# 56 late modulation chunks as VectorE products in the feed-forward stage instead of TensorE products

## The reference

```python
def _ada(cond, l, P):
    return (jax.nn.silu(cond) @ P['w_ada'][l] + P['b_ada'][l])[:, None, :]

def _layer(x, mod, l, P, pos, ctx):
    sm, scm, gm, sf, scf, gf = jnp.split(mod, 6, axis=-1)
    h = _rmsnorm(x, P['norm_mix_g'][l]) * (1 + scm) + sm
    a, own = _mixer(h, l, P, pos, ctx)
    x = x + gm * a
    h = _rmsnorm(x, P['norm_ffn_g'][l]) * (1 + scf) + sf
    f = _swiglu(h, ...) if l % 2 == 0 else _moe(h, l // 2, P)
    return x + gf * f, own
```

## Time and profile before

| | |
|---|---|
| median of 3 runs | 2117.39 us (2114.71 to 2118.08) |
| profiled execution, first to last instruction | 2115.9 us |
| granted TensorE clock, mean | 0.997 of full speed (2.4 GHz) |
| TensorE busy | 2061.1 us (97%) |
| VectorE busy | 1356.0 us (64%) |
| ScalarE busy | 1147.1 us (54%) |
| HBM traffic | 210 GB/s over the span |

### The profile page before, as it was taken

How to read it: one execution, slowest core, us unless ns; L and a number is a source line. 1 busy time by engine, 2 the same in 40 slices (tenths; PEclk the granted TensorE clock), 3 DMA queues, 4 the chain that set the end, 5 groups by cost and what they waited for, 6 DMA issues and landing times. The chain is left out here.

```text
span 2115.9 us, 31825 instructions
## 1 busy us (share of the span) xinstructions
PE 2061.1 (97%) x12214; PEld 1792.1 (85%) x12214; DVE 1356.0 (64%) x1435; ACT 1147.1 (54%) x1412; POOL 191.3 (9%) x186
## 2 busy tenths in 40 slices
PE   8999999999999999999999999999999999999997
PEld 4898568999999999989856887888888888888885
DVE  5427533643423444653853358988998889988898
ACT  5217544322212223532754347787877777878775
POOL 1130000000000000012000026200000000000003
PEclk9999999999999999999999999999999999999999
DMA  9220154234323222322024339999999999999996
GB/s 324 84 86 6 62 183 136 80 100 140 105 78 97 64 62 75 109 81 67 6 77 163 101 113 406 408 408 386 388 379 390 380 380 379 373 385 382 386 388 199
DMA packets 275056, 445.24 MB, mean 210 GB/s; under 512 B 11952, under 2 KB 158736, under 8 KB 274928
## 3 DMA queue, kind: packets, MB, share of 16 engines
q1 hardware_dynamic: 264480, 412.58, 54.4%
q0 software_dynamic: 8752, 30.09, 3.8%
q10 hardware_dynamic: 1728, 1.21, 0.2%
HBM read 428.34 MB, written 16.62 MB: 210 GB/s over the span
## 5 line engine op out<-in xcount | busy, mean ns | idle before, releaser
L1872 DVE TENSOR_TENSOR w_lo<-mraw,w_hi 128x1792 fp32r<-128x1792 f32 (+2 forms) x306 | 643.5, 2114 | 88.3 <-ACT w_hi L1226 87.1
L1226 ACT ACTIVATE w_hi<-mraw 128x1792 fp32r<-128x1792 f32 (+2 forms) x306 | 541.7, 1776 | 173.2 <-PE ps L2594 160.8
L2592 PE MATMUL ps<-w_hi,xs_lo 128*128 128x448 f32 (+1 forms) x816 | 310.6, 381 | 4.0 <-DVE w_lo L1872 2.9
L2594 PE MATMUL ps<-w_hi,xs_hi 128*128 128x448 f32 (+1 forms) x816 | 305.9, 375 | 0.0
L2593 PE MATMUL ps<-w_lo,xs_hi 128*128 128x448 f32 (+1 forms) x816 | 305.6, 374 | 0.0
L1348 DVE TENSOR_TENSOR sub_lo<-zone,sub_hi 128x1024 fp32r<-128x1024 f32 (+2 forms) x112 | 129.5, 1158 | 217.7 <-ACT sub_hi L909 217.7
L2592 PEld LDWEIGHTS ps<-w_hi,xs_lo 128*128 128x128 f32 x816 | 153.4, 188 | 30.3 <-DVE w_lo L1872 10.6
L1591 DVE TENSOR_REDUCE stat<-ps 128x2 f32<-128x1536 f32 (+3 forms) x80 | 92.3, 1156 | 121.7 <-PE ps L2275 100.9
L2594 PEld LDWEIGHTS ps<-w_hi,xs_hi 128*128 128x128 f32 x816 | 153.3, 188 | 19.7
L2593 PEld LDWEIGHTS ps<-w_lo,xs_hi 128*128 128x128 f32 x816 | 153.5, 188 | 18.7
L2143 PE MATMUL ps<-f_hi,sub_lo 128*128 128x320 f32 x704 | 162.7, 312 | 1.7 <-issue 1.7
(11 more groups left out here) (360 smaller groups left out, 3540.0 us busy)
## 6 DMA issues: line engine op xcount, KB each, us to landing
mraw<-in_moe_w_down SPq DMA_DIRECT2D x68, 1024.0 KB, 9.1
mraw<-in_moe_w_gate SPq DMA_DIRECT2D x68, 896.0 KB, 7.9
mraw<-in_moe_w_up SPq DMA_DIRECT2D x68, 896.0 KB, 7.4
zone<-in_w_ada SPq DMA_DIRECT2D x48, 1024.0 KB, 5.8
mraw<-in_moe_w_gate SPq DMA_DIRECT2D x34, 1024.0 KB, 7.9
mraw<-in_moe_w_up SPq DMA_DIRECT2D x34, 1024.0 KB, 9.5
mraw<-in_moe_w_down SPq DMA_DIRECT2D x34, 768.0 KB, 9.8
zone<-in_w_in SPq DMA_DIRECT2D x13, 1024.0 KB, 5.3
```

The lines of the kernel that those rows point to most:

```text
L1226: nc.scalar.activation(w_hi[:, n % SPLITS, a], mraw[:, n % MRING, a], ACT.Copy).then_inc(w_hi_ready, 1)
L1872: nc.vector.tensor_tensor(w_lo[:, n % SPLITS, a], mraw[:, n % MRING, a], w_hi[:, n % SPLITS, a].bitcast(f32), ALU.subtract).then_inc(w_spl ...
L2592: nc.tensor.matmul(out, a_lo, b_hi, start=start, stop=False)
L2594: return nc.tensor.matmul(out, a_hi, b_hi, start=False, stop=stop)
```

## The change

Layer 0's chunks 16 to 39 stay on TensorE (6 pairs, steps 0 to 12 of the attention of layer 0). The other 56 chunks, 40-47 of layer 0 and all 48 of layer 1, are computed by VectorE in the feed-forward stage of layer 0. The host lays their weights output-major: a chunk is 128 partitions (outputs) by 1024 inputs, and two chunks make a piece of 1 MB ("mods", 28 pieces, rows of 4 KB in memory). Both conditioning vectors are copied to all partitions by a DMA on ScalarE's queue in layer 0's second attention, and ScalarE applies SiLU to them (128 x 2048) at the start of the feed-forward stage. For each chunk VectorE does two products with a running sum, one for each vector, 112 in all, each 128 x 1024; the sum starts from the bias and goes right into `mod`. One chunk follows the low part in each of a block's two halves of VectorE's work; two chunks follow the low parts at each of columns 0 to 5 of the first half's down products. The pieces go into the same ring. Waits that named the old semaphores name the new one.

```diff
+ADA_COLS = 40 * P
+ADA_PAIRS = in_pairs([(0, c) for c in range(8, 20)])
+MODS = [(0, c) for c in range(40, 48)] + [(1, c) for c in (*range(8, 16), *range(8), *range(16, 48))]
+MODS_DOWN = 6
+def mods_at_down(d):
+    return len(FF_HALF[0]) + d
+def mods_at(j):
+    return j if j < len(FF_HALF[0]) else j + MODS_DOWN
 def weight_pieces():
...
-        for pair in ADA_PAIRS[l]:
+        for pair in ADA_PAIRS if l == 0 else ():
             out += [("ada", *p) for p in pair]
...
                     out += [("gate", j // 2), ("up", j // 2)]
-                    out += [("ada", *p) for p in ADA_FFN.get(j, ())]
-                out += [("down", half, d) for d in range(KC)]
+                    out += [("mods", mods_at(j)), ("mods", mods_at(j + 1))]
+                for d in range(KC):
+                    out.append(("down", half, d))
+                    if half == 0 and d < MODS_DOWN:
+                        out.append(("mods", mods_at_down(d)))
 def piece_freed(n):
...
+    if PIECES[n][0] == "mods":
+        return "mod_rows", 4 * (PIECES[n][1] + 1)
...
+                if kind[0] == "mods":
+                    sp.dma_start(slot.rearrange("p (c k) -> p c k", c=2), w_mods[:, 2 * kind[1]:2 * kind[1] + 2]).then_inc(arrival, 16)
+                    return
...
-            sp.wait_ge(mod_late, TURNS_BEFORE[1] + len(ADA_PAIRS[1]) // 2)
+            sp.wait_ge(mod_rows, 2 * len(MODS))
...
-                    pool.wait_ge(late_turned, TURNS_BEFORE[l])
+                    pool.wait_ge(mod_rows, 2 * len(MODS))
...
+                    if l == 0:
+                        act.dma_start(cond_rows.rearrange("p c k -> p (c k)"), d["cond_rows"].partition_broadcast(P)).then_inc(vec_in, 16)
...
                     root(4, token_scale)
+                    act.wait_ge(vec_in, 48)
+                    nc.scalar.activation(cond_rows, cond_rows, ACT.Silu).then_inc(cond_ready, 1)
...
+                def row_mods(m, i):
+                    n = PIECE_AT["mods", m]
+                    to, c = MODS[2 * m + i]
+                    dve.wait_ge(cond_ready, 2)
+                    dve.wait_ge(*piece_arrival(n))
+                    w = piece_place(n)[:, D_MODEL * i:D_MODEL * (i + 1)]
+                    b = V_BADA + 48 * to + c
+                    if m or i:
+                        dve.wait_ge(mod_rows, 4 * m + 2 * i - 1)
+                    for g in range(2):
+                        nc.vector.tensor_tensor_reduce(mod_parts if g == 0 else w, w, cond_rows[:, g], 1.0, vecs[:, b:b + 1],
+                                                       ALU.mult, ALU.add, mod[:, to, c, g:g + 1]).then_inc(mod_rows, 1)
...
                             sub_rest(q + 1 + (j == 0))
-                            if j - 1 in ADA_FFN:
-                                ffn_rows_turned(j - 1)
-                            if j - 2 in ADA_FFN and ffn_pair(j - 2) % 2:
-                                ffn_mods(j - 2)
+                            row_mods(mods_at(j), 0)
...
                             if j:
                                 sub_rest(q + 1)
+                            row_mods(mods_at(j), 1)
...
                                 sub_rest(q + 1)
+                            if half == 0 and d_ < MODS_DOWN:
+                                for i in range(2):
+                                    row_mods(mods_at_down(d_), i)
+                            if half == 0 and d_ == 0:
+                                dve.wait_ge(mod_rows, mods_before([(0, c) for c in range(40, 48)]))
                             residual(l, ("down", half, d_), d_, 40)
...
-                                if u == "gate" and j - 1 in ADA_FFN:
-                                    ffn_ada(j - 1)
-                                if u == "gate" and j - 2 in ADA_FFN and ffn_pair(j - 2) % 2:
-                                    ffn_turn(j - 2)
```

More of the change, by code:

```diff
@@ L86, with mods_before @@
 ADA_FIRST = (0, 2, 1, 3)
[L87 to L94, removed]
+ADA_COLS = 40 * P
+ADA_PAIRS = in_pairs([(0, c) for c in range(8, 20)])
+MODS = [(0, c) for c in range(40, 48)] + [(1, c) for c in (*range(8, 16), *range(8), *range(16, 48))]
+MODS_DOWN = 6
+def mods_before(chunks):
+    return 2 * (max(MODS.index(m) for m in chunks) + 1)
+def mods_at_down(d):
+    return len(FF_HALF[0]) + d
+def mods_at(j):
+    return j if j < len(FF_HALF[0]) else j + MODS_DOWN
 def weight_pieces():
@@ L310, in build @@
     w_ada = d["w_ada"].rearrange("l (k p) n -> l p k n", p=P)
+    w_mods = d["w_mods"].rearrange("c p k -> p c k")
     w_in = d["w_in"].rearrange("l (k p) n -> l p k n", p=P)
@@ L450, in build @@
         token_scale, up_part = spare[:, 0:T], spare[:, T:2 * T]
-        late_rows_t = arena[:, ATT + 1024 + RING * RING_F:ATT + 2048 + RING * RING_F].rearrange("p (u n) -> p u n", u=2)
+        cond_rows = arena[:, ATT + 1024 + RING * RING_F:ATT + 1024 + RING * RING_F + 2 * D_MODEL].rearrange("p (c k) -> p c k", c=2)
+        mod_parts = spare[:, 2 * T:2 * T + D_MODEL]
         shift_part = stat.rearrange("p i n -> p (i n)")[:, 0:8].rearrange("p (s u c) -> p s u c", s=2, u=2)
@@ L527, in build @@
         cond_ready, lam_exp, lam_prod_ready, mod_ready = sem("cond_ready"), sem("lam_exp"), sem("lam_prod_ready"), sem("mod_ready")
-        mod_late = sem("mod_late")
+        mod_late, mod_rows = sem("mod_late"), sem("mod_rows")
         ada_rows_done, ada_rows, late_rows, late_rows_done = sem("ada_rows_done"), sem("ada_rows"), sem("late_rows"), sem("late_rows_done")
@@ L806, in _ @@
                     pool.dma_start(slot_tokens, d["no_tokens"]).then_inc(no_tokens, 16)
-            pool.wait_ge(late_rows_done, PAIRS_BEFORE[1] + len(ADA_PAIRS[1]))
+            pool.wait_ge(late_rows_done, len(ADA_PAIRS))
+            pool.wait_ge(prompt_q, HEADS * DEPTH)
             nc.gpsimd.tensor_copy(router32, router_w[:]).then_inc(router_ready, 1)
@@ L1140, in _ @@
                     if k == 0:
-                        act.wait_ge(mod_late, TURNS_BEFORE[l] + len(ADA_PAIRS[l]) // 2)
+                        act.wait_ge(*((mod_rows, 2 * len(MODS)) if l else (mod_late, len(ADA_PAIRS) // 2)))
                     if l:
@@ L1655, in late_mods @@
                 def late_mods(v):
-                    dve.wait_ge(late_turned, TURNS_BEFORE[l] + v + 1)
-                    add_bias(l, 2 * ADA_PAIRS[l][2 * v][0][1], 8, ps[:, ADA_AT:ADA_AT + 16]).then_inc(mod_late, 1)
+                    dve.wait_ge(late_turned, v + 1)
+                    add_bias(0, 2 * ADA_PAIRS[2 * v][0][1], 8, ps[:, ADA_AT:ADA_AT + 16]).then_inc(mod_late, 1)
                 def late_rows_turned(u):
-                    dve.wait_ge(late_rows_done, PAIRS_BEFORE[l] + u + 1)
+                    dve.wait_ge(late_rows_done, u + 1)
                     nc.vector.transpose(ada_rows_t[:, u % 2], ps[:, ADA_AT:ADA_AT + 512]).then_inc(late_rows, 1)
@@ L1675, in beside @@
                         turned_lo(*turn_at(i - 1), turns_before(i - 1))
+                    if l or i // 5 >= len(ADA_PAIRS) // 2:
+                        return
                     if i % 5 == 1:
@@ L1687, in _ @@
                 sub_rest(q + 1)
-                dve.wait_ge(mod_late, TURNS_BEFORE[l] + len(ADA_PAIRS[l]) // 2)
+                dve.wait_ge(*((mod_rows, 2 * len(MODS)) if l else (mod_late, len(ADA_PAIRS) // 2)))
                 make_gain(l, 1)
@@ L1771, in _ @@
                                 sub_rest(q + 1)
+                            row_mods(mods_at(j), 1)
                         if half:
-                            dve.wait_ge(mod_late, TURNS_BEFORE[1])
+                            dve.wait_ge(mod_rows, mods_before([(1, c) for c in range(16)]))
                             make_gain(1, 0)
@@ L2420, in late_ada @@
                 def late_ada(u):
[L2422 to L2425, removed]
+                    pe.wait_ge(late_rows, u)
+                    pe.wait_ge(mod_late, u // 2)
+                    for p in ADA_PAIRS[u]:
                         ada(*p, ps[:, ADA_AT:ADA_AT + 512])
@@ L2429, in late_turn @@
                 def late_turn(v):
-                    pe.wait_ge(late_rows, PAIRS_BEFORE[l] + 2 * v + 2)
+                    pe.wait_ge(late_rows, 2 * v + 2)
                     sum_groups(ada_rows_t, ps[:, ADA_AT:ADA_AT + 16])
@@ L2435, in first @@
                 def first(i):
-                    if i % 5 == 4:
+                    if l == 0 and i % 5 == 4 and i // 5 < len(ADA_PAIRS) // 2:
                         late_turn(i // 5)
                 def beside(i):
-                    if i % 5 in (0, 2):
+                    if l == 0 and i % 5 in (0, 2) and i // 5 < len(ADA_PAIRS) // 2:
                         late_ada(2 * (i // 5) + (i % 5 == 2))
@@ L2455, in _ @@
                 else:
-                    pe.wait_ge(mod_late, TURNS_BEFORE[1] + len(ADA_PAIRS[1]) // 2)
+                    pe.wait_ge(mod_rows, 2 * len(MODS))
                     for c in range(2):
@@ L2468, in _ @@
```

(6 more changed lines are left out.)

## The result

The changed kernel takes 2131.05 us (median of 4 runs, 2130.58 to 2132.12), the kernel before, run beside it, 2117.73: a ratio of 1.0067, interval [1.0053, 1.0082]. It is 13.3 us slower, inside the range and on the side that was forecast, where 5 us had been the sum. The sum came out at the right sign partly because two of its errors cancel, so its terms are taken one by one.

The account below looks back on a forecast made before the run. TensorE was the bound by averages, but fed through VectorE, ScalarE and a three-slot weight ring. 33 us gained and 38 lost gave 5 us slower, 2117.4 + 5 = 2122 us; range 2108 to 2142.

Parts of the forecast that it names:

- The gain: Work leaving TensorE in layer 1's second attention, both attentions' last steps and the feed-forward stage: 33.0 us gained.
- the 15.9 us for six pairs and three turns: Layer 1's second attention: six pairs removed give 13.8 us and three turns 2.1, with TensorE still last in each step.
- The price x: VectorE's time per new product, taken as 1.30 us, between 1.15 and 1.44; the loss moves 84 us per us of it.
- The loss: Feed-forward stage of layer 0: 14 us in first-half blocks, 8 in the second half, 16 in down columns; 38 in all.
- The down columns: First half's down products: 2.4 us lost at each of five columns and 4 at the entry, 16 us.
- the chain: Transfer, split and products through the ring: 7.7 + 4x us per down column, 23.1 + 6x per two blocks.
- The first two blocks: Start of the feed-forward stage: the low part of gate 2 comes 3.4 us late, after block 0's products.
- The second half: Its 10 feed-forward blocks: 4.5 rounds of 2.4 us less 2.9 in hand, 8 us lost.
- the 38 that the prediction named as its sign: TensorE idle some 38 us in the feed-forward stage, about 2 at each of down columns 1 to 6, first half.
- The edits at nothing: Conditioning row's transfer, its SiLU (about 1.9 us, covered by VectorE's reciprocal) and moved GpSimd and SyncE waits: no cost.
- Rival (a): Feed-forward stage: a cheap product of 1.15 us, loss 25 us, total 2109 us, decided at 1.24 us; chance 0.25.
- Rival (b): Feed-forward stage: VectorE's free time takes all 146 us of products, TensorE never waits, 2084 us; chance 0.08.

Follow-up runs that it names:

- experiments 1 to 5: Variants of the changed kernel: additions removed 2088.17 us; products cut to 64 elements 2092.11; products on resident data 2092.49; no down-column pieces 2110.57; third product per chunk 2178.38.
- e6_no_down: Changed kernel without the six modulation pieces at the first half's down columns, their 24 products cut to 64 elements of resident data: 2110.57 us.
- e4_fill: Changed kernel with six unused TensorE products ahead of the second block and of down columns 1, 3 and 5 of the first half: 2132.34 us.
- e7_third: Changed kernel with a third full-size product, its result unused, ahead of the two of each chunk, no more bytes: 2178.38 us.
- the last kernel: Changed kernel with modulation chunks in their own place on GpSimd's queue, no product in the first block, three chunks moved to later down columns: 2092.65 us.

## Why the prediction came out as it did

**The gain: 29.1 for 33.0.** Layer 0 (2.9 for 3.1) and the feed-forward pairs (10.9) were right. Layer 1's second attention gave 15.3 for 19.0. The stage in the two traces, before and after:

```profile
1090.33:1178.16 87.83, 82.07 (x601) 57.03 (x600) 34.55 (x70) 47.65 (x98) 0.23 (x1) 1.00 0.56 192
```

```profile
1119.86:1192.44 72.58, 65.67 (x441) 53.32 (x440) 29.60 (x58) 47.09 (x98) 0.00 (x0) 1.00 0.00 1
```

TensorE's busy time fell by 16.4 us and its idle time grew by 1.2. The last steps gave the 3.1 us forecast; the term that was too large is the 15.9 us for six pairs and three turns, which gave 12.2. Its failed step is "with the pair gone TensorE itself is still the last one there": that was read from one step, and in others another wait ends last. TensorE's timeline before, then after:

```profile
1109.47 0.66 PE L2417 MATMUL ps<-ident,zone 128*128 128x128 f32 x4 [0.32 <-DVE h_lo L1650]
```

```profile
1128.55 1.56 PE L2306 MATMUL ps<-zone 96*128 96x256 f32 x4 [1.20 <-ACT zone L1072]
...
1136.14 0.66 PE L2448 MATMUL ps<-ident,zone 128*128 128x128 f32 x4 [0.32 <-DVE h_lo L1674]
1136.63 1.46 PE L2306 MATMUL ps<-zone 96*128 96x256 f32 x4
...
1140.89 1.46 PE L2306 MATMUL ps<-zone 96*128 96x256 f32 x4
...
1145.15 1.46 PE L2306 MATMUL ps<-zone 96*128 96x256 f32 x4
1148.88 1.46 PE L2306 MATMUL ps<-zone 96*128 96x256 f32 x4
...
1174.60 1.60 PE L2346 MATMUL ps<-zone 128*128 128x128 f32 x12 [0.93 <-ACT zone L1112]
```

Step by step, most of the 3.7 us that are missing lie in three places. At 1128.55 TensorE waits 1.2 us for ScalarE's exponentials (L1072), where the pair of the step before had covered them; that step is 1.4 us longer than before. Where the transposition waits for VectorE's low part of the group before, a step takes 4.26 us and not 3.73. The trace before has this wait once, at 1109.47; after, it stands at 1136.14, 1140.40 and 1144.66, and the two new ones take back 1.1 us. And the turn at 1156.25 gave nothing: without it TensorE waits 0.93 us for ScalarE's copy at 1174.60, where it had waited 0.75, and the step takes the same 3.86 us. The rest is spread over other steps. These waits were read from the traces; no run tests one of them apart.

**The price x: 1.205 for 1.30.** The scalar and the read-out cost nothing that shows. By the slope of the sum that is 84 x 0.095 = 8 us less loss: 30.

**The loss: 43.7 for 38, at the measured x for 30.** The mechanism is shown by experiments 1 to 5, and its slope held to 6% in all (the blocks fit, the columns grew less). These terms were too small:
- The down columns: 19.0 for 14 at the measured price. With the gaps filled 16.0 are left, so the chain is right to 2 us; the stretches at half clock add 3, because ScalarE then waits for the split weight that TensorE still holds. No step of the prediction let TensorE's idle time have a price beyond itself.
- The first two blocks: 6.0 us for 3.4. Work without transfers loses 5.6 of them, so it is the products ahead of low parts that are late already. I counted them, but from a lateness too small.
- The blocks of the first half: 30.6 to 31.5 us a pair for the chain's 30.3. The transfer of 5.2 us allows VectorE a wait of 1.05 for each mods piece. In the nine places it waits 9.5 us, 1.06 on average, but the four of blocks 4 to 10 have 1.4 on average, with one of 2.2. Why these are longer stays open.
- The second half: 7.2 us for 8, which looks right, but at the measured price its sum is 5.6. The distances are 30.2 to 30.8.

TensorE's idle time in the stage grew by 26 us, not by the 38 that the prediction named as its sign, and it came as one long gap every second down column, not as 2 us at each: part of the loss is matmuls at half clock, which count as busy.

**The edits at nothing** were nothing: the stages around them show no difference. Rival (a) would have come in had only its price decided, since x fell below its 1.24; the sum at the measured price was 3 us faster than before. That the kernel is slower is due to 3.9 us less gain and 13.7 us more loss than the sum has at that price. So the direction was forecast with a price that was too high, in place of a mechanism (the clock) that was missing and sizes that were too small. Rival (b) named 2084 us, and the two kernels that have the products outside the ring take 2093 and 2099; what it left out was above all the ring.

## What to carry to other kernels

Work on an engine with free time is cheap or dear by what its operands pass through: put in a ring that feeds the bound engine, its duration is added to the time in which a slot stays taken, and then to every round of the ring; with a place and a queue of its own the same work cost 6 us, at best, instead of 44. Find the round (transfer, preparation, use, free) and compare it with the bound engine's own round before looking at shares. And put no optional work where the stage starts, before what the bound engine already waits for.

## What the runs showed of the hardware

- The granted clock showed 0.50 for 7 us about each of four idle times of TensorE of 3.2 to 3.9 us in the changed kernel. In others it fell for half as long about idle times of 1.8 to 2.6 us (2.0 us at 549 and 1.8 at 723 in e6_no_down, 2.6 at 607 in e4_fill). But it stayed at 1.00 about 1.8 us at 487 in the changed kernel and 2.8 us at 632 in e7_third, so the length of one idle time doesn't decide it. With one unused product at each down column it was at 1.00 from 605 to 660 us.
- A fall cost 2 us a column where ScalarE waited for TensorE behind it, and at most 0.4 us where it didn't (e7_third's columns, the second block).
- The product with running sum costs 1.205 us for 1024 float32 elements and 0.205 for 64 (from one to the next), so 1.04 ns an element; the read-out of the sum takes 0.08 us beside it (0.14 behind a product into PSUM). With PSUM as its output it takes 1.287 us for 1.280, and the distance to the next is the same.
- 28 MB more in 500 us, from another queue than the weights, together with their products, cost 6.4 us by the stages of the last kernel against the removals alone, 4.5 by the medians. How much of it is the transfers was not measured.
